# Differential attention: wide and narrow query tiles in alternation, one place in the banks, value products ahead of the scores

## The reference

```python
def diff_attention(q, k, v, cos, sin, q_norm, k_norm, lam, lambda_init, subln):
    ...
    for blk in range(s // Q_BLOCK):                 # Q_BLOCK = 128
        q0, q1 = blk * Q_BLOCK, (blk + 1) * Q_BLOCK
        sc = jnp.einsum('bqhmd,bkhmd->bhmqk', q[:, q0:q1], k[:, :q1]).astype(jnp.float32)
        mask = (jnp.arange(q1) // CHUNK_2)[None, :] <= (jnp.arange(q0, q1) // CHUNK_2)[:, None]
        p = jax.nn.softmax(jnp.where(mask, sc, NEG_INF), axis=-1)
        w = p[:, :, 0] - lam * p[:, :, 1]
        outs.append(jnp.einsum('bhqk,bkhd->bqhd', w.astype(v.dtype), v[:, :q1]))
    o = jnp.concatenate(outs, axis=1)
    o = rms_norm_2(o, subln) * (1.0 - lambda_init)
```

## Time and profile before

| | us |
|---|---|
| median of 3 runs | 4943.58 |
| lowest and highest | 4936.13, 4952.0 |
| the profiled execution | 4941.17 |
| its span, first to last instruction | 4939.2 |
| TensorE busy | 4109.6 (83%) |
| VectorE busy | 2697.7 (55%) |
| ScalarE busy | 1996.0 (40%) |
| mean granted clock of TensorE | 0.909 |

### The profile page before, as it was taken

The page is one execution under the profiler, slowest core; times in us unless marked ns, Lnnn a source line. Parts: engine busy times, 40 slices in busy tenths (PEclk is TensorE's granted clock), DMA queues, the critical chain, the costliest instruction groups (busy, mean ns, idle before and its releaser), DMA issues. The chain is left out here.

```text
span 4939.2 us, 75219 instructions
## 1 busy us (share of the span) xinstructions
PE 4109.6 (83%) x30577; PEld 3081.4 (62%) x30577; DVE 2697.7 (55%) x4026; ACT 1996.0 (40%) x3406; POOL 466.9 (9%) x376
## 2 busy tenths in 40 slices
PE   6999876968886729999578998877789887399994
PEld 4888654458885608888466443756634655288883
DVE  4231154766664669999631554226610345399996
ACT  3111023645553307777431443226610223277773
POOL 0000012210002000111000330000000000111111
PEclk8999877979998859999789999989989988699997
DMA  5332312642223329999633231221021223599996
GB/s 195 132 134 91 116 50 69 192 143 82 78 77 133 137 97 407 391 398 392 238 115 122 74 110 63 102 99 52 27 85 51 102 60 119 225 405 411 412 410 253
DMA packets 363496, 845.89 MB, mean 171 GB/s; under 512 B 31711, under 2 KB 232447, under 8 KB 312726
## 3 DMA queue, kind: packets, MB, share of 16 engines
q1 hardware_dynamic: 342766, 782.71, 42.5%
q0 software_dynamic: 12032, 41.96, 2.6%
q10 hardware_dynamic: 8360, 16.47, 1.0%
HBM read 676.70 MB, written 164.35 MB: 170 GB/s over the span
## 5 line engine op out<-in xcount | busy, mean ns | idle before, releaser
L504 PE MATMUL psum<-proj_hi,proj_w 128*128 128x512 f32 (+2 forms) x1728 | 461.8, 356 | 15.3 <-DVE proj_w L544 13.8
L2657 DVE TENSOR_TENSOR moe_lo<-moe_raw,moe_hi 128x2048 fp32r<-128x2048 f32 x192 | 436.4, 2288 | 45.2 <-ACT moe_hi L2605 45.2
L4214 DVE TENSOR_TENSOR moe_lo<-moe_raw,moe_hi 128x2048 fp32r<-128x2048 f32 x192 | 428.2, 2284 | 32.8 <-ACT moe_hi L4169 32.7
L2605 ACT ACTIVATE moe_hi<-moe_raw 128x2048 fp32r<-128x2048 f32 x192 | 367.8, 1918 | 137.0 <-PE psum L2558 137.0
L4169 ACT ACTIVATE moe_hi<-moe_raw 128x2048 fp32r<-128x2048 f32 x192 | 356.9, 1910 | 40.1 <-PE psum L4130 40.1
L504 PEld LDWEIGHTS psum<-proj_hi,proj_w 128*128 128x128 f32 (+1 forms) x1728 | 304.1, 188 | 68.9 <-DVE proj_w L544 14.2
L2832 PE MATMUL psum<-qkv_w,hT 128*128 128x512 f32 x768 | 335.7, 596 | 13.4 <-DMA qkv_w<-in_w_in 13.4
L504 PE MATMUL psum<-proj_lo,proj_w 128*128 128x512 f32 (+2 forms) x864 | 306.3, 355 | 0.0
L2832 PEld LDWEIGHTS psum<-qkv_w,hT 128*128 128x128 f32 x768 | 145.5, 191 | 190.9 <-issue 176.9
L3420 PE MATMUL psum<-branches_T,mixed_w 128*128 128x512 f32 x512 | 222.8, 598 | 13.8 <-DMA mixed_w<-in_w_attn_o 13.8
L515 DVE COPY proj_out<-psum 128x512 f32<-128x512 f32 (+3 forms) x54 | 32.5, 602 | 355.6 <-PE psum L504 355.6
(11 more groups left out here) (623 smaller groups left out, 9023.0 us busy)
## 6 DMA issues: line engine op xcount, KB each, us to landing
moe_raw<-in_w_down SPq DMA_DIRECT2D x128, 1024.0 KB, 7.7
moe_raw<-in_w_gate_up SPq DMA_DIRECT2D x128, 1024.0 KB, 9.4
moe_raw<-in_w_gate SPq DMA_DIRECT2D x64, 1024.0 KB, 9.3
moe_raw<-in_w_up SPq DMA_DIRECT2D x64, 1024.0 KB, 9.9
uT<-proj_out SPq DMA_DIRECT2D x35, 640.0 KB, 3.0
chunks_pr<-prim SPq DMA_DIRECT2D x40, 512.0 KB, 4.0
proj_raw<-in_w_in SPq DMA_DIRECT2D x17, 1024.0 KB, 7.6
hT<-in_w_mod SPq DMA_DIRECT2D x32, 512.0 KB, 4.8
```

Source lines behind the costliest of these rows:

```text
L504: ins = nc.tensor.matmul(bank[e * nch + c][0:width, 0:n], l, r, start=(k == 0 and i == 0), stop=(k == KD - 1 and i == 2))
L2605: nc.scalar.activation(hi[:, n % R], raw[:, n % RAW], ACT.Copy).then_inc(s["hi_ready"], 1)
L2657: nc.vector.tensor_tensor(lo[:, n % R], raw[:, n % RAW], hi[:, n % R], ALU.subtract).then_inc(s["lo_ready"], 1)
L4214: nc.vector.tensor_tensor(lo[:, n % R], raw[:, n % RAW], hi[:, n % R], ALU.subtract).then_inc(s["lo_ready"], 1)
```

## The change

The order of the tiles of a head, and with it of every list, becomes 4, 0, 5, 1, 6, 2, 7, 3 (numbers from 0), that is 640, 128, 768, 256, 896, 384, 1024, 512 keys. `tile(j)` gives the tile's number in its head, `place(j)` where its result stands, so that `o` and `ss` are filled in the old order of places. The scores of all tiles now stand at one place in the banks, and the scores of tile j wait for the exponentials of j - 1 in every case. In TensorE's step the products of j - 2 come first, then the scores of j, then the transposes of j - 1. VectorE's step always has the weights of j - 1 first and then the maxima of j.

```diff
+        def tile(j):
+            return (4, 0, 5, 1, 6, 2, 7, 3)[j % NT]
+
+        def place(j):
+            return j - j % NT + tile(j)
+
         def wide(j):
-            return j % NT >= 4
+            return tile(j) >= 4
...
         def at(j, m):
-            i = j % NT
-            return 2 * m * BANK + (0 if wide(j) else (i % 2) * BANK)
+            return 2 * m * BANK
...
                 def scores(j):
-                    h, i = j // NT, j % NT
-                    if i == 0:
+                    h, i = j // NT, tile(j)
+                    if j % NT == 0:
                         pe.wait_ge(qkv_in[h % 2], 48 * (h // 2 + 1))
-                    free = j - 2 if 1 <= i < 4 else j - 1
-                    if free >= 0:
-                        pe.wait_ge(s["exp"], 2 * free + 2)
+                    if j:
+                        pe.wait_ge(s["exp"], 2 * j)
...
                 for j in range(STEPS):
+                    if 2 <= j <= J + 1:
+                        values(j - 2)
                     if j < J:
-                        if j % NT == 0 or wide(j):
-                            scores(j)
-                        if j % NT < 3:
-                            scores(j + 1)
+                        scores(j)
                     if 1 <= j <= J:
                         turn(j - 1)
-                    if 2 <= j <= J + 1:
-                        values(j - 2)
                     if pair_at(j, GROUPS_AT, 4):
                         columns_of(*pair_at(j, GROUPS_AT, 4))
...
-                    nc.scalar.activation(o[:, j % SLOTS_O, :], bank[6][:, 0:P], ACT.Copy, scale=rec[:, j, 0:1]).then_inc(s["o_ev"], 1)
+                    nc.scalar.activation(o[:, place(j) % SLOTS_O, :], bank[6][:, 0:P], ACT.Copy, scale=rec[:, j, 0:1]).then_inc(s["o_ev"], 1)
...
                 for j in range(STEPS):
-                    early = 1 <= j % NT < 4
-                    if early and j < J:
-                        maxima(j)
                     if 1 <= j <= J:
                         weights(j - 1)
-                    if not early and j < J:
+                    if j < J:
                         maxima(j)
```

More of the change, by code:

```diff
@@ L3146, in at @@
         def at(j, m):
-            i = j % NT
-            return 2 * m * BANK + (0 if wide(j) else (i % 2) * BANK)
+            return 2 * m * BANK
         def scores_of(j):
-            n = (j % NT + 1) * P
+            n = (tile(j) + 1) * P
             return [(a, min(a + BANK, n)) for a in range(0, n, BANK)]
@@ L3203, in turn @@
                 def turn(j):
-                    i = j % NT
+                    i = tile(j)
                     pe.wait_ge(s["w_ready"], j + 1)
@@ L3260, in evacuate @@
                 def evacuate(j):
-                    n = min(j % NT + 1, 4) * P
+                    n = min(tile(j) + 1, 4) * P
                     act.wait_ge(s["trA"], j + 1)
@@ L3269, in result @@
                         act.wait_ge(s["squared"], j)
-                    nc.scalar.activation(junk[:, :], bank[6][:, 0:P], ACT.Square, scale=rec[:, j, 0:1], accum_out=ss[:, j:j + 1])\
+                    nc.scalar.activation(junk[:, :], bank[6][:, 0:P], ACT.Square, scale=rec[:, j, 0:1], accum_out=ss[:, place(j):place(j) + 1])\
                         .then_inc(s["squared"], 1)
-                    nc.scalar.activation(o[:, j % SLOTS_O, :], bank[6][:, 0:P], ACT.Copy, scale=rec[:, j, 0:1]).then_inc(s["o_ev"], 1)
+                    nc.scalar.activation(o[:, place(j) % SLOTS_O, :], bank[6][:, 0:P], ACT.Copy, scale=rec[:, j, 0:1]).then_inc(s["o_ev"], 1)
                 def root(p):
@@ L3322, in evacuate @@
                 def evacuate(j):
-                    n = (j % NT - 3) * P
+                    n = (tile(j) - 3) * P
                     dve.wait_ge(s["trB"], nb(j + 1))
```

## The result

The changed kernel takes 5136.3 us (median of 4 runs, 5131.2 to 5140.7) where the kernel before takes 4940.3 beside it: a ratio of 1.0383, 95% interval 1.0367 to 1.0399. The two medians alone give 1.0397, or 196 us; against the kernel before in the later batches (medians of 4945.7 to 4947.8) the loss is 189 to 191 us, some 190 in what follows. The forecast was 5104, the range 5010 to 5135. Against its own reference of 4943.6 us the forecast is a ratio of 1.0325 and the upper end one of 1.0387: the measured ratio lies in the range, at its upper end, with an interval that reaches past it, and the measured time is 1.3 us above the range. The direction came out as forecast, and so did what makes the loss: the products on the chain and a lower clock. One of the two waits that the products bring with them was missed, and the stage takes 469 us where the forecast had 444.

What follows compares the result with a forecast made beforehand. It took one chain going round VectorE's maxima, ScalarE's exponentials and TensorE as the bound. Eight heads of 56.0 us, less about 4, gave 444 against 281.6; with a tail 1.5 shorter, +161 us: 5104, range 5010 to 5135.

Steps and rivals of the forecast that it cites:

- the products on the chain: Differential attention: products of j-2 wait for ScalarE's copy and hold up the scores; 42.2 us a head at full clock against 35.84.
- a lower clock: TensorE in the attention stage: idles of 2.6 to 3.6 us drop the clock; a head takes 56.0 us instead of 42.2.
- The rival on the other side: Attention stage: products fill TensorE's wait before the scores; head 32.9 us, stage -21 us, total 4923; chance 0.03.
- the signs that the prediction named: Profile after: TensorE idle ends at the copy, ScalarE's maxima wait over 120 us, head 56 us, stage clock near 0.6.
- the start of the products: TensorE step: products start after the copy, 0.70 us behind the second exponential's accumulator read; 0.40 to 0.60 for narrower tiles.
- 0.111 us a pass: Value products on TensorE at full clock: price per pass, two passes for each 128 keys; 0.213 at the low clock.
- the slow work: Products and scores at half clock: head 56.0 us, 80% of the way from fast to slow.
- all-slow: Every attention step at the low clock: +16.9 us, 59.1 us a head, total 5129; rival at 5120 to 5140, chance 0.12.
- a fall at each wide tile: TensorE clock in the attention stage: four falls in a head instead of about one, the clock back after about 5 us.
- a late fall: Start of a narrow attention step still fast where the clock falls late: 0.6 us given for it, an estimate.
- the first rival: Attention stage: chain right, but the clock holds for much of the time; total 4995 to 5060; chance 0.25.
- rule of every batch at the low clock: Attention stage: each pause makes the next matmuls start slow, so every step is slow; 5129 us, chance 0.12.

Runs made afterwards that it cites:

- the run with the result first: Changed kernel with ScalarE's result of j-2 moved ahead of the exponentials of j instead of behind the copy of j-1: 5073.4 us, ratio 1.0250.
- run with the result first and filler: Changed kernel with ScalarE's result of j-2 ahead of its exponentials and filler matmuls into bank 7, three per wide step, one per narrow: 5026.4 us, ratio 1.0161.
- map by map run: Kernel before with the scores' wait for the exponentials split by map, and VectorE taking map 0's maximum, the weights, map 1's maximum: 5011.8 us, ratio 1.0137.

## Why the prediction was right, and where its size was off

**Right: what the moved line does.** The products of j-2 stand on the chain, and each step of the chain had its length from a row: scores, maximum and exponentials agree with the round shown of the trace after to 0.01 us, and the order alone makes 182 us of the some 190. The rival on the other side, products that fill the wait before the scores, would have needed the copy ahead of T; the run that put it there got no gain: the copy delayed the exponentials, and the groups didn't fit the narrow rounds.

**Right: the clock falls.** The stage's granted clock went from 0.90 to 0.73, and filler alone gives 57 us back. Of the signs that the prediction named, ScalarE's wait for the maxima is up (285 us, over 120), but TensorE's idle doesn't end at the copy, the head has 58.9 us and not 56, and the clock is 0.73 and not near 0.6.

**Off: three terms of the sum.** The forecast had 444 us for the stage and it took 469. The chain at full clock, taken from 44.05 us a head without the second wait and 8 x 0.74 for it, is 50.0 us a head, 397 for the stage with 3 less for the first steps. So:
- the start of the products, set at 0.60 to 0.70 behind T, is 1.34 to 1.44. The step that failed is "those products wait for evA": it names one of the two waits. 62 x 0.74 = +46 us.
- the products were priced at 0.111 us a pass with nothing for their start after an idle: 0.2 us a group, with the handover some 0.23. 62 times, +14 us. (Products behind T in the run with the result first: 0.74 where the sum had 0.70.)
- the slow work was set at 80% of all-slow, 108 us. It is 469 - 397 = 72 us, 53% of the 135 (8 x 16.9) that all-slow would cost: -36 us. The 72 is a remainder and not a direct reading.

Together +24, and the miss is 25. The first would have been seen by reading every wait of the moved function and not only the one that speaks for the case. The third is where the forecast chose with the least to go by. Its own words were "a fall at each wide tile", four in a head, and 0.6 us for a late fall. The number was right: the trace's record of the clock has 34 falls between the first scores and the last T, 4.2 a head (before: 10). What a fall costs was too high. A row with its idle and the windows of the changed kernel show how it goes (transposes and idle at 3434.50 to 3438.42, then products, scores of a narrow tile from 3439.48):

```profile
3438.42 1.13 PE L3230 MATMUL psum<-attn_v,attn_wT 128*128 128x128 f32 x8 [3.26 <-ACT attn_o L3274]
```

```profile
3434.00:3438.00 4.00, 1.16 (x14) 0.83 (x10) 2.27 (x5) 2.48 (x8) 0.00 (x0) 1.00 0.00 0
3438.00:3439.80 1.80, 1.38 (x12) 1.29 (x14) 0.56 (x1) 0.28 (x2) 0.00 (x0) 0.99 0.00 0
3440.00:3446.00 6.00, 4.80 (x23) 3.85 (x21) 1.42 (x6) 1.90 (x8) 0.00 (x0) 0.50 0.84 262
3447.00:3450.00 3.00, 0.88 (x11) 0.57 (x7) 1.90 (x3) 1.29 (x3) 0.00 (x0) 1.00 0.00 0
3451.00:3463.00 12.00, 8.88 (x34) 6.66 (x36) 4.39 (x10) 5.25 (x14) 0.00 (x0) 0.50 0.00 1
```

TensorE stood idle for 3.26 us before 3438.42 and the clock was still at 2.4 GHz at the end of that idle and for over a microsecond of products; it fell near 3439.8, came back by 3447, fell again within the next idle, and was low from 3451 to 3463. Of the 34 falls 15 came within an idle and 19 behind one, up to 1.5 us into the work. So an idle is followed by slow work, but part of that work is often done before the fall, and the low stretches of over 6 and 12 us lie only in part over the chain. On the clock the first rival, that it holds for much of the time, was nearer than the forecast: its upper end is "a little over half" of the slow price. Its bracket (4995 to 5060) was left by the two missed terms: 4995 + 72 + 46 + 14 = 5127. The Trainium skill's rule of every batch at the low clock (TensorE: Matmul & The Clock Gate, "HAM oscillation — how this bites in real kernels") is not borne out here: there are idles of 3.3 to 4.3 us before 31 of the 62 groups of products and shorter ones before the others, and the work cost 53% of the slow price.

**By luck.** A term left out (46 us) and one overpriced (36) nearly cancel; that the time comes so near, at the edge of the range, is owed to that. With the second wait seen and the clock as I set it, the forecast would have been 5104 + 46 = 5150, above the range.

## What to carry to other kernels

Before a group is moved ahead in an in-order list, write down every wait at its head and where the other engine issues each of the things waited for; the last of them sets the price, and here it was the return of the one bank, behind a copy. Work placed "into the idle time" of an engine fills it only if its inputs are ready when the idle begins. Where TensorE idles for microseconds in every round, price the matmuls on the chain at both clocks, and try a filler matmul: it is a cheap test of what the clock costs, and sometimes the gain.

## What the runs showed of the hardware

Filler that TensorE does for nothing shortens the program: -57 us in the changed kernel (stage clock 0.73 to 0.97), and -0.28% in the kernel before (0.90 to 0.98), whose longest idle of TensorE from the first scores to the last T was 2.7 us.

A group of products behind an idle or a wait takes 0.20 us more than 0.111 a pass, whether it has 2 or 16 passes (run with the result first and filler, at full clock).

Matmuls with 64 rows, one map on the upper and one on the lower half of the array: 8 passes of 512 columns take 1.82 us together, 0.23 a pass, whether the maps alternate or stand one behind the other. One map's four passes take the same 1.82 us (3425.04 to 3426.86 in the map by map run), 0.45 a pass, about as long as the 128-row fillers (ten passes in 4.3 us). The Trainium skill says that row tiles of 64 work independently of each other (TensorEngine Tiling (Array Packing), section "Key Properties"); the 0.23 against 0.45 agrees with that. With the mask of map 0 between the maps, map 1 starts 0.97 us late in the wide tiles, where six passes stand ahead of it, and at once in the 512-wide tile, where four do. So neither the mask nor its signal alone keeps the halves apart; the number of passes ahead fits what all rows show, and wasn't tested by itself.
